# Long and short matmuls of a weight unit in groups of two, four or eight

## What is computed

```python
h = rmsnorm(x, g_mlp[l])
u = jnp.square(jax.nn.relu(jnp.einsum('bsd,df->bsf', h, w_ff1[l])))
x = x + jnp.einsum('bsf,fd->bsd', u, w_ff2[l])
```

## Time and profile before

| | |
|---|---|
| Time, median of 3 runs | 2438.38 us |
| The runs | 2449.64, 2438.1, 2438.38 us |
| Span of the profiled execution | 2447.4 us |
| TensorE busy | 2433.9 us, 99% |
| VectorE busy | 1573.0 us, 64% |
| ScalarE busy | 1168.0 us, 48% |
| HBM read | 445.41 MB, 183 GB/s over the span |

### The profile page before, as it was taken

How to read it: one execution, slowest core, us unless ns; L and a number is a source line. 1 busy time by engine, 2 the same in 40 slices (tenths; PEclk the granted TensorE clock), 3 DMA queues, 4 the chain that set the end, 5 groups by cost and what they waited for, 6 DMA issues and landing times.

```text
span 2447.4 us, 32332 instructions
## 1 busy us (share of the span) xinstructions
PE 2433.9 (99%) x13637; PEld 2108.0 (86%) x13637; DVE 1573.0 (64%) x1578; ACT 1168.0 (48%) x1308; POOL 0.2 (0%) x4
## 2 busy tenths in 40 slices
PE   8999999999999999999999999999999999999999
PEld 7788888888888888888888888888888888888887
DVE  6565665665666566566556767857777677656763
ACT  5454444554444344344344555545554455435542
POOL 0000000000000000000000000000000000000000
PEclk9999999999999999999999999999999999999999
DMA  7556556565556665665665555555665666566653
GB/s 237 164 156 198 154 189 187 185 185 190 184 180 194 190 206 177 194 190 189 186 195 177 185 181 164 171 177 186 180 190 187 176 196 189 184 186 187 184 189 129
DMA packets 236764, 449.64 MB, mean 184 GB/s; under 512 B 16433, under 2 KB 19627, under 8 KB 236619
## 3 DMA queue, kind: packets, MB, share of 16 engines
q1 hardware_dynamic: 235851, 446.44, 58.4%
q10 hardware_dynamic: 768, 1.14, 0.1%
HBM read 445.41 MB, written 2.11 MB: 183 GB/s over the span
## 4 chain that ended last, share of the span: by engine, by line
PE 96%; DVE 2%; ACT 1%; DMA 0%; issue 0%; SPq 0%; DVEq 0%; ACTq 0%
PE PS L69 96%; DVE WL L69 1%; ACT WH L69 0%; DVE TA L69 0%; DMA RAW<-in_w_in 0%; DVE TB L69 0%; ACT XHL L69 0%; DVE TC L69 0%; ACT TA L69 0%; DVE PB L69 0%; SPq L69 0%; ACT TB L69 0%; DVE K L69 0%; DVE SEL L69 0%; DVE MHL L69 0%
## 5 line engine op out<-in xcount | busy, mean ns | idle before, releaser
L69 DVE TENSOR_TENSOR WL<-RAW,WH 128x1024 fp32r<-128x1024 f32 (+1 forms) x844 | 1021.3, 1220 | 709.4 <-ACT WH L69 709.1
L69 PE MATMUL PS<-XHL,WH 128*128 128x512 f32 x3984 | 1400.8, 397 | 2.8 <-DVE WL L69 2.0
L69 ACT ACTIVATE WH<-RAW 128x1024 fp32r<-128x1024 f32 (+1 forms) x845 | 881.1, 1053 | 927.9 <-PE PS L69 920.7
L69 PE MATMUL PS<-XHL,WL 128*128 128x256 f32 x3968 | 1111.3, 280 | 0.0
L69 PEld LDWEIGHTS PS<-XHL,WH 128*128 128x128 f32 x3984 | 746.2, 187 | 185.6 <-DVE WL L69 2.7
L69 PEld LDWEIGHTS PS<-XHL,WL 128*128 128x128 f32 x3968 | 748.9, 189 | 0.3
L69 PE MATMUL PS<-MHL,WH 128*128 128x512 f32 x2000 | 699.4, 395 | 1.0 <-DVE TA L69 1.0
L69 PE MATMUL PS<-MHL,WL 128*128 128x256 f32 x2000 | 559.1, 280 | 0.0
L69 PEld LDWEIGHTS PS<-MHL,WH 128*128 128x128 f32 x2000 | 374.9, 187 | 89.1 <-DVE TA L69 1.4
L69 PEld LDWEIGHTS PS<-MHL,WL 128*128 128x128 f32 x2000 | 377.2, 189 | 0.1
L69 DVE TENSOR_TENSOR TA<-TA,PS 128x1024 f32<-128x1024 f32 x72 | 87.9, 1221 | 7.9 <-ACT TA L69 0.5
(11 more groups left out here) (149 smaller groups left out, 973.9 us busy)
## 6 DMA issues: line engine op xcount, KB each, us to landing
RAW<-in_w_ff SPq DMA_DIRECT2D x256, 512.0 KB, 4.3
RAW<-in_w_in SPq DMA_DIRECT2D x224, 512.0 KB, 3.8
RAW<-in_w_up SPq DMA_DIRECT2D x176, 512.0 KB, 4.1
RAW<-in_w_down SPq DMA_DIRECT2D x88, 512.0 KB, 4.2
RAW<-in_w_mix_out SPq DMA_DIRECT2D x32, 512.0 KB, 4.5
RAW<-in_w_out SPq DMA_DIRECT2D x32, 512.0 KB, 4.4
RAW<-in_w_conv_out SPq DMA_DIRECT2D x16, 512.0 KB, 3.8
RAW<-in_w_attn_out SPq DMA_DIRECT2D x16, 512.0 KB, 4.6
```

Source lines behind the costliest of these rows:

```text
L69: ins = step[1](*step[2], **step[3])
```

## The change

feature_item takes a word for the order of a unit's matmuls. h stands for a long matmul, l for a short one, and the digits for the bank:

- "one" (as before): h0 l0 h1 l1 h2 l2 h3 l3, and the same for the second chunk
- "two": h0 h1 l0 l1 h2 h3 l2 l3, and the same for the second chunk
- "four": h0 h1 h2 h3 l0 l1 l2 l3, and the same for the second chunk
- "all": eight h (both chunks, four banks each), then eight l

Segment 0 of the feed-forward part takes "two", segment 1 "four", segment 2 "all", segment 3 "one", each for w_ff1 and w_ff2. All other feature items keep "one". In every feature item the waits for both chunks of the source now stand ahead of the unit's first matmul, where the wait for the second chunk stood ahead of that chunk's matmuls. The start flag goes to the first matmul of a bank in the group, the stop flag to its last, and the only increment to the last of the unit.

```diff
--- before.py
+++ after.py
@@ -316,7 +316,21 @@
             turn[0] ^= 1
             return s, b
 
-        def feature_item(parts, src, tok, mid=(), small=False):
+        def turn_about(nk, nb):
+            return [(x, k, j) for k in range(nk) for j in range(nb) for x in "hl"]
+
+        def four_by_four(nk, nb):
+            return [(x, k, j) for k in range(nk) for x in "hl" for j in range(nb)]
+
+        def two_by_two(nk, nb):
+            return [(x, k, j) for k in range(nk) for j0 in range(0, nb, 2) for x in "hl" for j in range(j0, min(j0 + 2, nb))]
+
+        def all_by_all(nk, nb):
+            return [(x, k, j) for x in "hl" for k in range(nk) for j in range(nb)]
+
+        walks = {"one": turn_about, "four": four_by_four, "two": two_by_two, "all": all_by_all}
+
+        def feature_item(parts, src, tok, mid=(), small=False, order="one"):
 
             s, b = side() if small else take()
             mid = dict(mid)
@@ -324,16 +338,17 @@
                 split_to(u)
                 PE.wait([split_done[u]])
                 h, l = wview(WH, u), wview(WL, u)
-                for k, kc in enumerate(kcs):
+                for kc in kcs:
                     PE.wait([need(kc, tok)])
-                    for j, bank in enumerate(banks):
-                        st = first and k == 0
-                        en = last and k == len(kcs) - 1
+                walk = walks[order](len(kcs), len(banks))
+                for n_w, (what, k, j) in enumerate(walk):
+                    kc, bank = kcs[k], banks[j]
+                    if what == "h":
                         PE.do(mm, PS[:, b + bank, :], h[:, k, j * P:(j + 1) * P], src[:, kc, :],
-                              start=st, stop=False, inc=False)
-                        end = j == len(banks) - 1 and k == len(kcs) - 1
+                              start=first and k == 0, stop=False, inc=False)
+                    else:
                         t = PE.do(mm, PS[:, b + bank, 0:T], l[:, k, j * P:(j + 1) * P], src[:, kc, 0:T],
-                                  start=False, stop=en, inc=end)
+                                  start=False, stop=last and k == len(kcs) - 1, inc=n_w == len(walk) - 1)
                 hl_free[u] = t
                 split_to(u + AHEAD)
                 pump()
@@ -935,6 +950,7 @@
             later(rest())
 
         nxt = {}
+        orders = ("two", "four", "all", "one")
         for seg in range(4):
             utok = {}
             for g in range(4):
@@ -943,11 +959,11 @@
                     SP.dma(nc.sync.dma_start, K2[:], bass.AP(ERD.tensor, ERD.offset, [[1, P], [384, 8], [1, T]]), s_wp,
                            after=[er_t, branches_t])
                 mid = {4: [lambda: norm_plain("r2", [TB], ["acc"])]} if seg == 0 and g == 0 else {}
-                it = feature_item(wide(io["w_ff1"][0], 0, ALLK, 2048 * seg + 512 * g), XHL, xtok, mid)
+                it = feature_item(wide(io["w_ff1"][0], 0, ALLK, 2048 * seg + 512 * g), XHL, xtok, mid, order=orders[seg])
                 later(ff_evac(it, g, "r2", utok))
             for g in range(4):
                 mid = {5: [bias_item]} if seg == 1 and g == 0 else {}
-                it = feature_item(wide(io["w_ff2"][0], 2048 * seg, ALLK, 512 * g), MHL, utok, mid)
+                it = feature_item(wide(io["w_ff2"][0], 2048 * seg, ALLK, 512 * g), MHL, utok, mid, order=orders[seg])
                 later(final_evac(it, g, nxt) if seg == 3 else residual_evac(it, g, None, None, None))
         xtok = nxt
```

## The result

| | before | changed |
|---|---|---|
| Median of 7 runs | 2438.64 us | 2446.03 us |
| Fastest, slowest | 2437.8, 2449.64 us | 2444.89, 2457.67 us |
| Span of the profiled execution | 2447.4 us | 2443.7 us |
| Ratio changed / before | | 1.0042, 95% interval 1.0024 to 1.0061 |

The forecast was 3.3 us faster.

A forecast was written before the change was run, and what follows sets the result against it. TensorE's pace between matmuls was taken as the bound: 1088 x (346.7 - 226.7 - 117) ns = 3.3 us gained, hoisted waits 0, so 2438.4 - 3.3 = 2435 us; range 2426 to 2452 us.

The forecast's parts named there:

- What bounds the kernel: Whole kernel: TensorE, busy 2433.9 of 2447.4 us; only how fast it goes between matmuls can move the end.
- LL: Regrouped units, passage from long matmul to long: taken as 226.7 ns from the token items, upper end 232.
- SS: Regrouped units, passage from short matmul to short: taken as 117 ns, ends 110 and 120.
- The passages at the turns: Each group's one long-to-short and one short-to-long passage: together 346.7 ns, taken as unchanged.
- The beat handed on: Segment 3, old order, inheriting 353.3 ns a pair in place of 346.7: 3.4 us, counted only in a rival.
- slower rival: Segments 0 to 2 at 353.3 ns a pair, 10.2 us, and segment 3 inheriting it, 3.4 us: 2452 us; chance 0.17.
- The faster rival: Regrouped segments: short matmuls close up to the weight load's 110 ns, 10.9 us gained, 2427.5 us; chance 0.13.
- Hoisted wait: Feature items, waits for both source chunks ahead of the unit: bounded to 0 to 2 us, taken as 0.
- releases: End of each unit: the last matmul still carries the only increment, so loads and splits keep their times.
- Same bank: Neighbouring matmuls, grouped, write different banks: no fixed cost seen apart, counted inside the ends of the sum.
- The spread as 212 units on the slow beat: Three runs of before: spread of 11.3 us guessed as 212 units at 353.3 ns a pair, 53.3 ns a unit.
- The signs: Feed-forward trace: runs of longs at 227 ns, shorts at 117, forecast half times; wrong if their sum leaves 337 to 352 ns.

The follow-up runs named there:

- experiment 1: Changed kernel with all four segments back in the old order, only the hoisted waits left: 2439.71 us, ratio 1.0009 to before.
- experiment 6: Changed kernel with all four segments in an order where each short matmul comes one long one later (h0 h1 l0 h2 l1 ...): 2450.37 us, ratio 1.0037.
- Experiments 10 to 12: Kernel before plus f32 matmuls of constants: 192 columns behind every attention, norm, bias and token item, 256 there, or three of 192 only: 2432.92, 2434.13, 2431.22 us.

## Why the prediction was wrong

- *What bounds the kernel.* Right: nothing but TensorE's rhythm moved, and DVE and ACT followed.
- *LL.* Right: 226.7 ns taken, 226.7 measured in steady state with these operands.
- *SS.* This is the step that failed first. "The nearest row is the passage short to long, 117 ns ... I take 117": measured 120.0. The row read was half of a pair (230 + 117) in which 3 ns are shifted from the short passage to the long one, so it can't be added to an LL of another stretch. The argument given for the upper end (columns and a fixed 13.3 ns each) was the one that holds, and by it the term is 1088 x 0.0: the 3.3 us of gain were not there.
- *The passages at the turns*, "together 346.7 ns as now (taken as unchanged)". This is what gave the result its sign. With LL + SS at 346.7, the turn and what it leaves behind came to 350.0, 363.3 and 366.7 ns in groups of 2, 4 and 8, so 64 x (13.3 + 33.3 + 20.0) ns = 4.3 us in the three segments; 4.0 us of it show against rows 3, since five units there were still on the slow beat. The prediction gave this passage no range. Why TensorE needs several long matmuls behind a turn to settle is not shown.
- *The beat handed on.* The sum had it at nothing. The slower rival had it with its size, 64 x 53.3 ns = 3.4 us, and that is what segment 3 shows. Its other part, the three regrouped segments on the slow beat for 10.2 us, did not come: they have rhythms of their own for 4.3 us. The rival's total of 2452 us was thus 6 us too high. It was said to decide once LL + SS passed 360 or the beat was passed on; it was passed on without the first. With SS, the turns and this, 3.3 + 4.0 + 3.4 us lie between the 3.3 us gained in the forecast and the 7.4 us lost.
- *The faster rival.* Wrong: short matmuls do not close up to 110 ns. The Trainium skill's gap of an isolated matmul ("TensorE: Matmul & The Clock Gate", Back-to-back issue gap), 216 and 109 ns, is 11 ns below both steady sizes here, and the trace does not agree with it for these operands.
- *Hoisted wait, releases.* Right at nothing (experiment 1).
- *Same bank.* At nothing in steady streams, as experiment 6 sets out; its part in the choice of the beat is open.
- *The spread as 212 units on the slow beat.* It was called a guess. Experiments 10 to 12 bear it out: the spread goes with the beat of the last stretch, 226 units.
- *The signs.* The one named for being wrong, LL + SS outside 337 to 352 ns, stayed silent: in the unit of "all" shown above the seven passages between longs average 230.7 ns and the seven between shorts 119.0, together 349.7. The halves did speak: forecast 88.4 (beside its 2.0 us), 88.2, 88.1 and 88.75 us, measured 89.17 (the second half), 89.82, 89.39 and 90.45. Segment 3 away from 88.75 was named as the sign that the slow beat had come, and it had.
- *The range* held the result and "same" by 0.5% was right, but by the width of the range, not by the mechanism: the likeliest time lay on the wrong side by 11 us.

## What to carry to other kernels

When steady streams of each kind show the same fixed price over the columns, reordering has nothing to gain, and what it can change is the turns; size them from a steady run of each kind and treat the passage between kinds as an unknown of its own. A row that is half of an alternation is not the price of a passage: add up whole periods. Where TensorE is the bound and unit periods come in two values, look for what stands ahead of each stretch: here three small matmuls in the right places took off 6 us or more against the quickest runs of before, about what the change moved, and none of their five runs fell into the group some 11 us slower.

## What the runs showed of the hardware

- A stream of one long and one short fp32r matmul, the same instructions on the same engine at the same clock, runs at 346.7 or at 353.3 ns a pair. In the traces it kept its beat over 200 units and more while DVE, ACT and the DMAs worked beside it, and changed it only at another kind of matmul or another order of the same ones.
- A foreign f32 matmul can set it anew: 192 and 256 columns gave the fast beat 12 times in 12, 32 columns the slow one 6 times in 6. A kick that finds the fast beat costs about 0.33 us with what it leaves behind (in the trace with 192-column kicks behind every foreign item the units around it took 2.964 and 2.911 us, against 2.773). Why these sizes do it was not tried.
- At a turn from short to long fp32r matmuls the longs come late, up to 236 ns apart, and reach 226.7 only after five to seven; the shorts behind longs start at 114 and reach 120.
- A weight load rides under the matmul ahead of it even when all are short: 169 short matmuls with a load each stood 120.0 ns apart.
